# Expert rows gathered set by set in turn, and every V set summed on TensorE

## The reference

```python
q = (xc @ w_query).reshape(PEER_CHUNK, PEER_HEADS, 2, PEER_SUBKEY_DIM)   # 128 tokens, 8 heads
s = jnp.einsum('chpd,hpnd->chpn', q, sub_keys)
s1, i1 = lax.top_k(s[:, :, 0], 16);  s2, i2 = lax.top_k(s[:, :, 1], 16)
cand = s1[..., :, None] + s2[..., None, :]
best, flat = lax.top_k(cand.reshape(128, 8, 256), 16)
experts = e1 * 128 + e2                       # e1, e2 from i1, i2 at flat
g = jax.nn.softmax(best, axis=-1)
act = gelu(einsum('cd,chkd->chk', xc, take(u, experts)))
out = einsum('chk,chkd->cd', g * act, take(v, experts))
h = h + out
```

## Time and profile before

| what | us |
|---|---|
| median of 3 runs | 1595.07 |
| lowest and highest | 1591.04 to 1599.96 |
| span of the profiled execution | 1554.8 |
| first gather issued | 217.2 |
| last addition of a V set ends | 953.4 |
| last sum of PE ends | 955.1 |

### The profile page before, as it was taken

How to read it: one execution, slowest core, us unless ns; L and a number is a source line. 1 busy time by engine, 2 the same in 40 slices (tenths; PEclk the granted TensorE clock), 3 DMA queues, 4 the chain that set the end, 5 groups by cost and what they waited for, 6 DMA issues and landing times.

```text
span 1554.8 us, 17801 instructions
## 1 busy us (share of the span) xinstructions
PE 1233.7 (79%) x6525; PEld 893.8 (57%) x6525; DVE 1047.1 (67%) x1923; ACT 426.1 (27%) x738; POOL 572.7 (37%) x626
## 2 busy tenths in 40 slices
PE   6988896667876564575556558999999999999997
PEld 4555574234443221232222225989989999899996
DVE  5767467878588666775665564677776777656556
ACT  1145313021102100200210113333335555344332
POOL 4100016667776666767777774010010000000000
PEclk9996898779888776877787779999999999899999
DMA  9834148999999999999999999678848556355561
GB/s 329 341 121 152 34 178 309 376 363 368 389 396 377 346 379 394 379 362 388 382 368 360 390 358 344 208 269 303 288 150 297 176 168 206 128 162 190 197 207 69
DMA packets 179710, 435.47 MB, mean 280 GB/s; under 512 B 13881, under 2 KB 84610, under 8 KB 179638
## 3 DMA queue, kind: packets, MB, share of 16 engines
q0 software_dynamic: 84384, 306.26, 51.9%
q1 hardware_dynamic: 94214, 126.18, 24.3%
q10 hardware_dynamic: 1040, 2.10, 0.4%
HBM read 433.44 MB, written 2.14 MB: 280 GB/s over the span
## 4 chain that ended last, share of the span: by engine, by line
PE 59%; DMA 14%; POOL 11%; DVE 8%; issue 6%; ACT 2%; SPq 0%; DVEq 0%; POOLq 0%
PE quad L1429 14%; PE quad_a L1383 8%; PE quad L1383 7%; PE quad_a L1534 7%; DMA arena<-in_peer_v_dram,arena 6%; POOL arena L745 6%; PE quad_a L1443 6%; DMA ring<-in_peer_v_dram,arena 5%; POOL ring L745 5%; PE quad_a L1139 3%; PE quad_a L1235 2%; PE quad L1217 2%; PE quad_a L1611 2%; DMA ring<-in_ffn_w_gu_dram 2%; PE quad_a L1599 1%
## 5 line engine op out<-in xcount | busy, mean ns | idle before, releaser
L1383 PE MATMUL quad_a<-arena 128*128 128x512 f32 x384 | 202.2, 691 | 147.6 <-DMA arena<-in_peer_v_dram,arena 147.6
L1383 PE MATMUL quad<-ring,arena 128*128 128x512 f32 x360 | 191.1, 695 | 111.5 <-DMA ring<-in_peer_v_dram,arena 108.1
L1383 PEld LDWEIGHTS quad_a<-arena 128*128 128x128 f32 x384 | 84.6, 225 | 264.6 <-issue 264.3
L745 POOL DMA_INDIRECT ring<-in_peer_u_dram,arena x136 | 137.8, 1013 | 206.2 <-DVE arena L2006 130.8
L1383 PEld LDWEIGHTS quad<-ring,arena 128*128 128x128 f32 x360 | 79.6, 226 | 216.0 <-issue 216.0
L1429 PE MATMUL quad<-u_hi,w_hi 128*128 128x256 f32 x704 | 199.1, 283 | 2.0 <-DVE u_lo L1926 2.0
L1429 PE MATMUL quad<-u_lo,w_hi 128*128 128x256 f32 x704 | 199.1, 283 | 0.0
L1429 PE MATMUL quad<-u_hi,w_lo 128*128 128x256 f32 x704 | 198.9, 283 | 0.0
L1884 DVE TENSOR_TENSOR w_lo<-ring,w_hi 128x2048 fp32r<-128x2048 f32 x66 | 150.7, 2289 | 52.0 <-ACT w_hi L929 51.7
L697 POOL DMA_DIRECT2D arena<-in_w_ada_dram x60 | 31.8, 531 | 400.2 <-DVE arena L1677 395.3
L2026 DVE CUSTOM_DVE_ANT_0 arena<-ring,quad 128x1024 f32<-128x1024 f32 x128 | 154.7, 1220 | 35.3 <-DMA ring<-in_peer_u_dram,arena 19.1
(11 more groups left out here) (364 smaller groups left out, 2257.2 us busy)
## 6 DMA issues: line engine op xcount, KB each, us to landing
ring<-in_ffn_w_gu_dram SPq DMA_DIRECT2D x44, 1024.0 KB, 9.3
arena<-in_w_ada_dram POOLq DMA_DIRECT2D x60, 512.0 KB, 6.4
ring<-in_ffn_w_down_dram SPq DMA_DIRECT2D x22, 1024.0 KB, 5.0
ring<-in_w_mix_in_dram SPq DMA_DIRECT2D x20, 1024.0 KB, 6.3
arena<-in_peer_w_query_dram SPq DMA_DIRECT2D x4, 2048.0 KB, 7.9
ring<-in_w_ada_dram POOLq DMA_DIRECT2D x12, 512.0 KB, 10.5
arena<-in_w_in_dram SPq DMA_DIRECT2D x3, 2048.0 KB, 35.2
arena<-in_w_out_dram SPq DMA_DIRECT2D x2, 2048.0 KB, 10.8
```

Of the source, the lines that this page charges most:

```text
L745: gp.indirect_dma_start(out=rows_of(n), out_offset=None, in_=t["peer_" + kind][0], in_offset=bass.IndirectOffsetOnAxis(ap=expert[tt][:, sl ...
L1383: last = te.matmul(sum_side[tt][:, cols], diag[:, i % DIAGS], rows_of(n)[:, cols], start=(slot == pe_slots[0]), stop=(slot == pe_slots[-1] ...
```

## The change

The order of the gathers is written set by set: eight U sets first, then one U set and one V set in turn (slot `at` of u, slot `at - 8` of v), and at the end the last eight V sets. Since buffers go by `n % 8`, U sets now lie in buffers 0, 2, 4, 6 and V sets in 1, 3, 5, 7, save for the first and the last eight. U set 8g+7 has number 16g+6 and V set 8g number 16g+9; before, they were 16g-1 and 16g+16.

PE sums all 128 slots of a tile; DVE's additions of V sets, and their waits, are gone, and ACT writes 64 more diagonals. DVE's order in a group becomes: the gates of the group before, four dots, routing, four dots, and after the last group of a tile `add_sum`. ACT takes the square root for tile 1's norm ahead of the GELU of its group and not behind it. SP's wait for set 510 stays the same number, and nothing else is moved.

```diff
@@ -214,25 +214,21 @@
-        SETS = [("u", 0)]
-        for g in range(1, QT * GROUPS):
-            SETS += [("u", g), ("v", g - 1)]
-        SETS += [("v", QT * GROUPS - 1)]
-        first_set = {group: GB * i for i, group in enumerate(SETS)}
+        SETS = [("u", 0, slot) for slot in range(GB)]
+        for at in range(GB, QT * SLOTS):
+            SETS += [("u", *divmod(at, SLOTS)), ("v", *divmod(at - GB, SLOTS))]
+        SETS += [("v", *divmod(at, SLOTS)) for at in range(QT * SLOTS - GB, QT * SLOTS)]
+        set_at = {name: n for n, name in enumerate(SETS)}
 
         def set_of(kind, tt, slot):
 
-            return first_set[kind, tt * GROUPS + slot // GB] + slot % GB
+            return set_at[kind, tt, slot]
...
-        def on_pe(tt, slot):
-
-            return slot % 4 != 3
-
-        pe_slots = [slot for slot in range(SLOTS) if on_pe(0, slot)]
+        pe_slots = list(range(SLOTS))
@@ -729,23 +725,20 @@
-            for kind, group in SETS:
-                tt, first = group // GROUPS, group % GROUPS * GB
-                if (kind, group) == ("v", GROUPS):
+            for n, (kind, tt, slot) in enumerate(SETS):
+                if (kind, tt, slot) == ("v", 1, 0):
                     final_scale(0)
                 for i, (piece_tile, head, _) in enumerate(PIECES):
-                    if kind == "u" and (tt, first) == (piece_tile, head * TOPK):
+                    if (kind, tt, slot) == ("u", piece_tile, head * TOPK):
                         pool.wait_ge(routed.sem, i + 1)
-                for slot in range(first, first + GB):
-                    n = set_of(kind, tt, slot)
-                    if n >= GB:
-                        used(pool, n - GB)
-                    elif n == 6:
-                        pool.wait_ge(d_full.sem, d_at["wo", 1, 1] + 1)
-                    gp.indirect_dma_start(out=rows_of(n), out_offset=None, in_=t["peer_" + kind][0],
-                                          in_offset=bass.IndirectOffsetOnAxis(ap=expert[tt][:, slot:slot + 1], axis=0)).then_inc(rows_ld[n % GB], 16)
...
+                if n >= GB:
+                    used(pool, n - GB)
+                elif n == 6:
+                    pool.wait_ge(d_full.sem, d_at["wo", 1, 1] + 1)
+                gp.indirect_dma_start(out=rows_of(n), out_offset=None, in_=t["peer_" + kind][0],
+                                      in_offset=bass.IndirectOffsetOnAxis(ap=expert[tt][:, slot:slot + 1], axis=0)).then_inc(rows_ld[n % GB], 16)
@@ -955,9 +946,9 @@
             for group in range(QT * GROUPS):
-                gelu_group(group)
                 if group == NORM1_AT:
                     root(("h1", 1))
+                gelu_group(group)
@@ -1373,8 +1364,6 @@
             def sum_group(group):
                 tt, first = group // GROUPS, group % GROUPS * GB
                 for slot in range(first, first + GB):
-                    if not on_pe(tt, slot):
-                        continue
@@ -2032,21 +2021,8 @@
-            own_before = [None]
-
-            def add_row(tt, slot):
-                n = set_of("v", tt, slot)
-                landed_set(ve, n)
-                if own_before[0] is not None:
-                    used(ve, own_before[0])
-                own_before[0] = n
-                v.scalar_tensor_tensor(out=hx[:, tt], in0=rows_of(n), scalar=gate[tt][:, slot:slot + 1], in1=hx[:, tt],
-                                       op0=ALU.mult, op1=ALU.add).then_inc(rows_used[n % GB], 1)
-
             def add_sum(tt):
                 used(ve, set_of("v", tt, pe_slots[-1]))
-                if own_before[0] is not None:
-                    used(ve, own_before[0])
                 step(v.tensor_tensor(hx[:, tt], hx[:, tt], sum_side[tt], ALU.add))
@@ -2060,14 +2036,13 @@
             for group in range(QT * GROUPS + 1):
                 tt, first = group // GROUPS, group % GROUPS * GB
+                if group:
+                    gate_group(group - 1)
+                    tb, fb = (group - 1) // GROUPS, (group - 1) % GROUPS * GB
                 if group < QT * GROUPS:
                     if first == 0:
                         ve.wait_ge(hn_in_psum.sem, tt + 1)
-                    dot_rows(tt, range(first, first + 2))
-                if group:
-                    gate_group(group - 1)
-                if group < QT * GROUPS:
-                    dot_rows(tt, range(first + 2, first + GB))
+                    dot_rows(tt, range(first, first + 4))
                 if group in KEYS_AT:
                     top_keys(*KEYS_AT[group])
...
                 if group == NORM1_AT:
                     normed(1)
+                if group < QT * GROUPS:
+                    dot_rows(tt, range(first + 4, first + GB))
                 if group:
-                    tb, fb = divmod(group - 1, GROUPS)
-                    for slot in range(fb * GB, fb * GB + GB):
-                        if not on_pe(tb, slot):
-                            add_row(tb, slot)
-                    if fb == GROUPS - 1:
+                    if fb == SLOTS - GB:
                         add_sum(tb)

```

More of the change, by code:

```diff
@@ L628, in first @@
                     elif f == 0 and n == 2:
-                        landed_set(sp, len(SETS) * GB - 2)
+                        landed_set(sp, len(SETS) - 2)
                     elif f == 0:
@@ L731, in _ @@
             pool.wait_ge(a_full.sem, a_at["ps", 0, 1] + 1)
[L732 to L734 removed]
+            for n, (kind, tt, slot) in enumerate(SETS):
+                if (kind, tt, slot) == ("v", 1, 0):
                     final_scale(0)
                 for i, (piece_tile, head, _) in enumerate(PIECES):
[L737 removed]
+                    if (kind, tt, slot) == ("u", piece_tile, head * TOPK):
                         pool.wait_ge(routed.sem, i + 1)
[L739 to L748 removed]
+                if n >= GB:
[4 more added lines that the diff above has]
+                                      in_offset=bass.IndirectOffsetOnAxis(ap=expert[tt][:, slot:slot + 1], axis=0)).then_inc(rows_ld[n % GB], 16)
+            for n in range(len(SETS) - GB, len(SETS)):
                 used(pool, n)
```

1 line of the change is left out of this document (removed).

## The result

| | before, us | changed, us | changed / before, 95% interval |
|---|---|---|---|
| the measurement, 11 runs each | 1599.96 | 1608.30 | 1.0067 (1.0046 to 1.0088) |
| again, second chip, 11 and 6 runs | 1556.92 | 1544.50 | 0.9924 (0.9905 to 0.9944) |
| again, third chip, 14 and 10 runs | 1591.14 | 1597.74 | 1.0047 (1.0025 to 1.0070) |

What follows compares the result with a forecast made beforehand. The prediction took the gather stage as DMA-bound (98% busy), with dips from a starved queue. Terms -23 + 0 + 3 - 4 + 3 + 2 = -19, taken as 20, gave span 1535 plus 40.3: 1575 us, range 1550 to 1604.

Steps and rivals of the forecast that it cites:

- part 1: Gather stage, U and V sets in turn: the dip goes, 14 plain cycles fall from 22.45 to 20.8 us, 23 us gained.
- what lies around it: Time outside the profiled span: 1595.07 - 1554.8 = 40.3 us, taken to stay and added to the forecast span of 1535.
- part 5: Gates first in DVE's order: some 0.6 us a group, hidden; at the start two dots come later, 3 us lost.
- part 3: Groups 2 to 9, tile 1's queries on PE: cycles counted unchanged, bounds -11 us and +27 us.
- part 4: Routing after the fourth dot: two cycles with picks lose 3 us, five with searches gain 4 us.
- part 6: The tail, last eight sets all V: PE ends 5 us after the last landing, now 3.0, 2 us lost.
- nothing gained: Second rival, chance 0.20: the gather rate is the DMA engines' own, dips only move, 22.5 us a cycle, 1595 to 1600 us.
- Part 2: The sums: DVE loses 64 additions, 82 us, off the path; PE gains 64 slots, hidden when fast; counted as 0.
- The prediction's own sign of being wrong here: POOL waiting for dots for more than some 25 us in all would show part 4 too small.
- The third rival: Chance 0.15: PE turns into the gather stage's bound; with half of its slots cold, 1621 us.

Runs made afterwards that it cites:

- e13: The changed kernel, unchanged, run again on a chip where the kernel before takes 1591.14 us: 1597.74 us, 1.0047 of the kernel before.
- e0: The kernel before, with no edit, profiled once more: 1588.28 us, span 1586.6 us.
- e5: The changed kernel with tile 1's query matmuls and key scores laid between PE's sums of the same group: 1541.94 us, 0.9904 of the kernel before.
- e3: The changed kernel with DVE's old order (two dots, gates, six dots, routing): 1689.25 us, 1.0599 of the kernel before.
- the best kernel: The changed kernel with queries laid between PE's sums and dots between routing steps: 0.9765 and 0.9940 of the kernel before on two chips.
- e14: The changed kernel with queries laid between PE's sums and dots between routing steps, on e13's chip: 1580.19 us, 0.9940 of the kernel before.

## Why the prediction was wrong, by its own steps

**The step that failed** is in part 1: "a V set 1.9 us on a fast PE [...]; what is left [...] still holds the 6.4 us from a gather's issue to its landing", the wait from which the largest term, -23 us, came. On the kind of chip that was measured PE is fast (granted clock 0.96 in the stage), but it releases many V sets late: POOL stood for over 1 us behind 27 of them, 61 us in all, and the plain cycles took 22.8 to 23.2 us where the sum has 20.8. The prediction's own numbers leave 10.4 - 1.9 - 6.4 = 2.1 us of slack, and a release that comes 2 to 5 us late is more than that. (On a cold PE the 6.1 us left would not have held the 6.4 us either, though the text says so.)

What let it pass is "what lies around it is 1595.07 - 1554.8 = 40.3 us [...] and stays". 1.7 us lie around a span. The other 38.6 us are the difference of two kinds of chip, so the stalls were read on one kind and taken off a time of the other. This step alone moves no number: it cancels in the forecast, which is 1595.07 - 20 whatever the span.

| from the first gather to the last sum, us | forecast | second kind | first kind (e13 against e0) |
|---|---|---|---|
| to the 33rd gather (part 5) | +3 | +1.4 | -1.4 |
| sets 32 to 176 (part 3) | 0 | +5.5 | +12.1 |
| sets 176 to 320 (part 4, rest of part 1) | some -6 | -3.6 | -0.9 |
| sets 320 to 496 (11 cycles of part 1) | -18 | -19.1 | -0.3 |
| from there to the last sum (part 6) | +2 | +3.6 | +2.0 |

(e13's first gather also starts 2.2 us earlier than e0's, which is not in the table.) On the second kind the change takes 12.4 us off 1556.92, where 20 were forecast: right in sign, and 8 us too much, which lie between sets 32 and 320 (+1.9 us where parts 1, 3 and 4 together have some -6). On the first kind it added 8.3 us in the measurement and 6.6 us on the third chip.

**Part 1, the plain cycles**, was right on the kind of chip that it was read from: 1.65 us a cycle forecast, 1.73 measured, 20.69 us where 20.8 stood, 404 GB/s over 227.56 us. So the DMA engines' own rate was not the limit, and the rival "nothing gained" is refuted there. On the first kind the plain cycles did gain nothing, as that rival said, but not for its reason: the gathers moved 409 GB/s from 904.5 to 911 us. The Trainium skill, page "SBUF — State Buffer", section "A bandwidth-pool intuition that's wrong (but worth ruling out)", has about 358 GB/s for a core from HBM; the 11 cycles on the second kind exceed it too. The cause is only in part what part 1 says. Of the 19.1 us, the waits for V sets (beyond POOL's usual 0.3 us) give 10.3, from 12.4 to 2.1, and the gathers themselves, no longer drawn out by DVE's additions, give 11.5, from 14.2 to 2.7 us above 0.95 us each; 2.3 us of waits for dots come on top. On the first kind the waits for V sets rise from 16.4 us to 27.1 in e13 and undo the 11.3 us that the shorter gathers give there. A turn of the buffers is 8 x 1.25 = 10.0 us, of which the changed kernel on the second kind needs 7.1 (median of the stage) from a V gather to its slot, 1.95 for the slot and 0.27 to the next gather, so less than 1 us is to spare.

**Part 2, the sums** "off the path" was wrong for the additions: they stood on POOL's path, with the 11.5 us above. The 0 for both halves also hides that each alone loses: the sums alone 43 us on the second kind (bursts of eight), the order alone 1.6 to 2.0% on the first (additions behind routing). In the changed kernel on the second kind PE is 75% busy in plain cycles at a clock of 0.99, where 66% stood, since a slot by itself takes 1.95 us and not 1.72; it hides all the same. The Trainium skill, same page, section "Who interferes with whom", lets an instruction with two SBUF inputs contend with GpSimd, and the traces agree: 47 gathers over 1.1 us before, 39 of them beside an addition, 8 in the changed kernel on the second kind, 35 with the additions in the new order.

**Part 3, the queries:** 0 forecast. For sets 32 to 176, with the pick in group 6 among them, it is +5.5 us on the second kind and +12.1 to +13.7 on the first, within the bounds of part 3. Most of it is not the queries': on the second kind the waits for dots in this part are 19.4 us and those for V sets 6.5. On the first kind (e13 against e0) the waits for dots are 14.3 us against none and those for V sets 28.5 against 23.3, while the shorter gathers give back 7.

**Part 4, routing in the middle,** was the term that was mis-sized on the second kind. A pick was priced at 4.7 us lost and makes POOL wait 5.7 (6.00 less the usual 0.30) in groups 6 and 12, but 2.9 in group 19; the searches were priced at 1 us each and mostly cost 1.6 to 3.1 us at the fifth dot. All waits for DVE are 44.0 us against 10.3 before (1.9 for dots, 8.4 for additions), where the sum had 3 - 4 = -1 us for this part. The prediction's own sign of being wrong here, over 25 us of waits for dots, came on both kinds (34.5 us on the first). Spread out, this term and the queries are worth 22 us by the medians (25 us in the windows), of which the queries alone (e5, on another chip) make some 3.

**Part 5:** from the first gather to the 33rd it is 54.9 us against 53.5, +1.4 where 3 stood. The wait before the diagonals was hidden, as said; e3 hints how narrowly, some 85 us being lost on the first kind with the gates two dots later and routing last.

**Part 6, the tail,** +2 forecast: from the last gather's start to the end of the last sum 13.5 us against 8.8, +4.7. The overhang was right: PE ends 5.5 us after the last landing, where 5 stood, against 3.0 before. What was left out is that the last gather itself lands 8.0 us after its start, against 5.8 before, as landings take 7.2 us in the plain cycles too, against 6.4 before. PE works through the end without a pause, nine slots of 1.74 us:

```profile
925.17 15.69 PE L1372 MATMUL quad_a<-arena 128*128 128x512 f32 x36 [0.60 <-DMA arena<-in_peer_v_dram,arena]
...
927.40 0.95 POOL L738 DMA_INDIRECT arena<-in_peer_v_dram,arena  x1 [0.36 <-PE quad_a L1372]
```

The third rival (PE bound, cold) is refuted on both kinds: the clock was 0.95 and more in each third of the stage. The 1608 us lie near the times of rivals two and three, but come from neither's mechanism.

## What to carry over

Subtract a profile's span from its own run's time before a difference is called overhead; when the two don't belong together, the profile may be from another chip, and a stall priced there need not be the stall at home. Work out how much a buffer has to spare in a turn, and set the longest hold seen against it, not only the usual one. An order that leaves each buffer under 1 us to spare gains where releases are prompt and gains nothing where one in some 18 sets comes 4 us late. When a consumer's work is moved next to a fast-turning buffer, break its long blocks up: here blocks of up to 9 us of routing between two dots, spread together with the queries, gave 22 us where the change itself gave 12.

## What was not expected of the hardware

The kernel before had medians of 1600, 1594 and 1591 us on the first kind and 1556.7 and 1556.9 on the second, and nearly all of the difference lies in the gather stage: what comes before it took 215 to 218 us and what comes behind the last sum 596 to 604 us on both, in all kernels.

On the first kind some of PE's releases come 2 to 5 us after its matmuls, two within 0.06 us of each other, and "remote" waits appear in POOL's table (23 us before, 60.4 changed, 70.5 in the best kernel); on the second kind no profile has any. PE's query matmuls, which wait for nothing, show gaps of 1.0 and 1.1 us there too while the DMA engines move 376 GB/s, so PE itself is held at times; but before the late release at 910.34 the matmuls keep starting 2.6 us apart (904.15, 906.71, 909.27), so there only the release is late. DVE's are not: in the measured profile 45 of 164 recorded releases of PE come over 1 us late, and all of the 131 recorded ones of DVE within 0.02 us.

In the plain part the late releases come mostly 23 to 27 us apart (797.1, 823.0, 848.7 us), and of the 27 and 26 V sets behind which POOL stood in the two profiles of the changed kernel on the first kind, 17 are the same sets; sets 423, 441 and 459 are among them in e14 too, at other times. So they depend on the place in the program and not on the moment. The traces of the first kind also lack part of the semaphore records (of 8,192 landings, 16 to a set, 3,535 are there in the measured profile, and all in those of the second kind); whether what loses them also delays PE is not shown.

What holds PE is open: no run here varied the load on memory at a fixed order of PE's work, and each chip of the experiments was met in one session, so a trait of the chip cannot be told from another load on it or a state that it was in.
